# The first feed-forward block: down product in Strassen's scheme, and the modulation work spread over it

## What is computed

```python
def swiglu(h, w_gate, w_up, w_down):
    return (jax.nn.silu(h @ w_gate) * (h @ w_up)) @ w_down
...
    for l in range(DEPTH):
        shift1, scale1, gate1, shift2, scale2, gate2 = jnp.split(c_act @ ada_w[l] + ada_b[l], 6, axis=-1)
        if l == N_A_LAYERS:
            k_shift, k_scale = jnp.split(c_act @ kv_ada_w + kv_ada_b, 2, axis=-1)
...
        h = modulate(rms_norm(x, norm2_g[l]), shift2, scale2)
        x = x + gate2[:, None, :] * swiglu(h, ffn_w_gate[l], ffn_w_up[l], ffn_w_down[l])
```

## Time and profile before

| | us |
|---|---|
| median of 3 runs (1119.43 to 1123.12) | 1123.01 |
| the profiled execution | 1123.41 |
| its span | 1121.6 |
| PE busy in the span | 1059.0 (94%) |
| DVE busy in the span | 577.9 (52%) |
| first block on PE, from first gate product to last down product | 136.94 to 367.16 |
| second block on PE | 512.67 to 721.15 |

### The profile page before, as it was taken

The page is one execution under the profiler, slowest core; times in us unless marked ns, Lnnn a source line. Parts: engine busy times, 40 slices in busy tenths (PEclk is TensorE's granted clock), DMA queues, the critical chain, the costliest instruction groups (busy, mean ns, idle before and its releaser), DMA issues.

```text
span 1121.6 us, 21217 instructions
## 1 busy us (share of the span) xinstructions
PE 1059.0 (94%) x9229; PEld 910.9 (81%) x9229; DVE 577.9 (52%) x1112; ACT 295.6 (26%) x709; POOL 64.0 (6%) x84
## 2 busy tenths in 40 slices
PE   6878999999999999889999999999997899999997
PEld 4647888888888867678999999988886688887786
DVE  8986455344421727727766575335823551602632
ACT  6512410000000645623010000133322341202641
POOL 3010010110100100000000000000003000000000
PEclk9899999999999999999999999999998999999999
DMA  9995879999945334073544552443440003644220
GB/s 290 363 310 176 300 257 370 346 329 358 329 184 189 108 116 152 31 226 122 178 152 154 181 186 84 142 151 113 131 151 4 4 4 117 203 157 124 76 76 37
DMA packets 128742, 195.78 MB, mean 175 GB/s; under 512 B 4176, under 2 KB 114394, under 8 KB 122250
## 3 DMA queue, kind: packets, MB, share of 16 engines
q1 hardware_dynamic: 118218, 131.15, 36.7%
q0 software_dynamic: 10144, 62.92, 14.8%
q10 hardware_dynamic: 288, 0.36, 0.1%
HBM read 191.53 MB, written 1.05 MB: 172 GB/s over the span
## 4 chain that ended last, share of the span: by engine, by line
PE 82%; DVE 12%; ACT 3%; issue 2%; DMA 0%; SPq 0%; DVEq 0%; ACTq 0%
PE psum L743 48%; PE psum L1129 11%; PE psum L1215 7%; PE psum L1183 6%; DVE arena L1942 4%; PE psum L1018 2%; PE psum L1721 1%; ACT arena L2978 1%; DVE sq L1942 1%; DVE arena L1948 1%; DVE arena L2112 1%; PE psum L1696 1%; DVE arena L2206 1%; ACT sq L2978 1%; DVE arena L1945 1%
## 5 line engine op out<-in xcount | busy, mean ns | idle before, releaser
L2978 ACT ACTIVATE arena<-psum 128x512 f32<-128x512 f32 (+6 forms) x229 | 102.6, 475 | 574.6 <-PE psum L743 379.3
L743 PE MATMUL psum<-hT,ring 128*128 128x256 f32 x1072 | 239.4, 380 | 2.2 <-DVE hT L1948 1.3
L743 PEld LDWEIGHTS psum<-hT,ring 128*128 128x128 f32 x1072 | 201.3, 190 | 32.8 <-issue 6.5
L743 PE MATMUL psum<-arena 64*64 64x64 f32 (+6 forms) x2252 | 91.8, 252 | 16.4 <-issue 11.6
L1942 DVE TENSOR_TENSOR arena<-arena 128x512 f32<-128x512 f32 (+8 forms) x141 | 94.9, 696 | 11.3 <-PE psum L1183 8.6
L743 PE MATMUL psum<-hT,arena 128*128 128x256 f32 (+2 forms) x664 | 95.4, 323 | 4.9 <-DVE hT L1942 4.8
L743 PEld LDWEIGHTS psum<-hT,arena 128*128 128x128 f32 (+2 forms) x664 | 83.4, 180 | 16.5 <-issue 6.7
L743 PEld LDWEIGHTS psum<-arena 64*64 64x64 f32 (+3 forms) x2252 | 72.2, 150 | 30.3 <-issue 26.4
L743 PE MATMUL psum<-ring,arena 128*128 128x256 f32 (+2 forms) x288 | 73.3, 415 | 0.5 <-ACT arena L2978 0.5
L743 PEld LDWEIGHTS psum<-ring,arena 128*128 128x128 f32 x288 | 54.5, 190 | 18.1 <-issue 7.7
L1942 DVE TENSOR_TENSOR arena<-arena,psum 128x512 f32<-128x512 f32 (+2 forms) x56 | 30.7, 569 | 73.4 <-ACT arena L2978 41.1
(11 more groups left out here) (312 smaller groups left out, 1469.3 us busy)
## 6 DMA issues: line engine op xcount, KB each, us to landing
aring<-in_ada_w POOLq DMA_DIRECT2D x36, 1024.0 KB, 8.4
ring<-in_a_w_in SPq DMA_DIRECT2D x14, 1024.0 KB, 5.4
arena<-in_ffn_w_gate SPq DMA_DIRECT2D x12, 1024.0 KB, 5.4
arena<-in_ffn_w_up SPq DMA_DIRECT2D x12, 1024.0 KB, 8.3
ring<-in_ffn_w_down SPq DMA_DIRECT2D x11, 1024.0 KB, 6.8
ring<-in_ffn_w_gate SPq DMA_DIRECT2D x10, 1024.0 KB, 8.8
ring<-in_ffn_w_up SPq DMA_DIRECT2D x10, 1024.0 KB, 9.2
ring<-in_ada_w POOLq DMA_DIRECT2D x8, 1024.0 KB, 14.5
```

The lines of the kernel that those rows point to most:

```text
L743: return eng.matmul(dst, w, x, start=first, stop=last)
L2978: return eng.activation(dst, x, f, **k)
```

## The change

Layer 0 joins `HALVED`, with `FAST[0]` empty: its gate and up products stay whole (`whole_chunks`), and only its down product goes by Strassen's scheme, after all gates rather than between them. `swiglu` is gone from all engines. The calls of `ada_panel` are put at new places, 22 beside the gates and 14 beside the down product. Group 6 is summed in `acc` in place of `sq`. ACT copies the modulation columns out of PSUM (`take_columns`), and `ada_bias` adds the bias in SBUF. In both blocks the right-hand sums of the last three steps (8, 9, 10) are made by one `combine_hidden` behind the last step; before, the second block made those of steps 8 and 9 within step 10.

```diff
-        HALVED = (1,)
+        HALVED = (0, 1)
+        FAST = {0: (), 1: tuple(range(1, NDN))}
...
-                    n, nth, pool = unit_of(l, j), nth_of(l, j), "ab"[j % 2]
+                    n, nth, pool = unit_of(l, j), nth_of(l, j), "ab"[FAST[l].index(j) % 2]
...
+            ROWS_AT, COLUMNS_AT = {3: 3, 7: 4, 9: 5}, {4: 3, 8: 4, 10: 5}
...
+            def ada_beside_down(i, q):
+
+                if (i, q) == (2, 0):
+                    ada_rows(6)
+                if (i, q) == (2, 2):
+                    row_columns(6, row_late, "a")
+
+            swiglu_of_halves(0, 0, ada_beside, ada_beside_down)
...
                 for j in range(1, NDN):
+                    if j not in fast:
+                        for m in range(2):
+                            c = 2 * j + m
+                            combine_to(j + 1, m + 1)
+                            eng.wait_ge(*filled_at(("gu", l, c)))
+                            eng.wait_ge(done("silu_ready"), silus(l, c))
+                            tt(hid[:, c, :], hid[:, c, :], bank_of(("gu", l, c))[:, T:2 * T], ALU.mult)\
+                                .then_inc(*v.empties(("gu", l, c)))
+                            hid_done[0] = v.last
+                            beside(j, 1)
+                        combine_to(j + 1, 3)
+                        if j % 2 == 0 and j < NDN - 1:
+                            combine_hidden(l, [j - 2, j - 1])
+                        beside(j, 0)
+                        if j == NDN - 1:
+                            combine_down(l, 0)
+                            combine_down(l, 1)
+                        continue
...
-                combine_hidden(l, [NDN - 1])
+                combine_hidden(l, [8, 9, 10])
...
-                combine_down(l, 2)
-                combine_down(l, 3)
-                ahead = 4
+                ahead = 2
                 for i in range(KC // 2):
                     for d in range(ahead, min(3 * i + 6, DOWN_PANELS * KC // 2)):
                         combine_down(l, d)
+                        beside_down(i, d)
                     ahead = 3 * i + 6
+                    beside_down(i, None)
                     down_outputs(i)
...
-            def ada_beside(c):
-                for _ in range(2 if c < 14 else 1):
+            def ada_beside(j, n):
+                if n == 2 or j == 9:
+                    return
+                if n:
                     ada_panel()
-                if c in (7, 11, 15, 19):
-                    ada_bias({7: 3, 11: 4, 15: 5, 19: 6}[c])
-            swiglu(0, ada_beside)
+                elif j in (3, 6):
+                    ada_panel()
+                if n == 0 and j in (6, 10):
+                    ada_bias({6: 3, 10: 4}[j])
+
+            def ada_beside_down(i, d):
+                if d is not None:
+                    ada_panel()
+                else:
+                    for _ in range((0, 0, 1, 3)[i]):
+                        ada_panel()
+                    if i in (1, 3):
+                        ada_bias(5 if i == 1 else 6)
```

More of the change, by code:

```diff
@@ L2273, in combine_weights @@
                 g, u = slot(at), slot(at + 1)
-                s1, s2, s4 = [unit_sums(j)[:, x] for x in range(3)]
+                s1, s2, s4 = [unit_sums(l, j)[:, x] for x in range(3)]
                 if part == 1:
@@ L2340, in first_chunks, with swiglu_of_halves, combine_to @@
                 eng.wait_ge(*filled_at(("gu", l, 1)))
-                eng.wait_ge(done("silu_ready"), silu_base(l) + 2)
+                eng.wait_ge(done("silu_ready"), silus(l, 1))
                 tt(hid[:, 1, :], hid[:, 1, :], bank_of(("gu", l, 1))[:, T:2 * T], ALU.mult)\
                     .then_inc(*v.empties(("gu", l, 1)))
-            def swiglu_of_halves(l, h_base, behind):
+            def swiglu_of_halves(l, h_base, behind, beside=lambda j, n: None, beside_down=lambda i, d: None):
+                fast = FAST[l]
+                parts = [(j, part) for j in fast for part in range(1, 5)]
+                sent = [0]
+                def combine_to(j, part):
+                    while sent[0] < len(parts) and parts[sent[0]] <= (j, part):
+                        combine_weights(l, *parts[sent[0]])
+                        sent[0] += 1
@@ L2369, in swiglu_of_halves @@
+                    if ahead:
+                        combine_to(j + 1, 2)
                     eng.wait_ge(done("first_copied"), copy_of(l, j))
@@ L2390, in swiglu_of_halves @@
                     tt(hid[:, two, half_1], ps(p5), u2, ALU.add).then_inc(*v.empties(p5))
-                    if j < NDN - 2:
-                        combine_weights(l, j + 2, 1)
+                    if j + 2 in fast:
+                        if ahead:
+                            combine_to(j + 2, 1)
+                    beside(j, 1)
                     eng.wait_ge(*filled_at(p7))
@@ L3193, in swiglu_of_halves @@
                 for j in range(1, NDN):
+                    if j not in FAST[l]:
+                        for c in (2 * j, 2 * j + 1):
+                            eng.wait_ge(*filled_at(("gu", l, c)))
+                            act(hid[:, c, :], bank_of(("gu", l, c))[:, 0:T], ACT.Silu).then_inc(*s.signals("silu_ready"))
+                        beside(j)
+                        continue
                     nth, two = nth_of(l, j), slice(2 * j, 2 * j + 2)
```

214 lines of the change are left out of this document (98 added, 116 removed).

## The result

The changed kernel takes **1135.82 us** (median of 6 runs, 1134.93 to 1142.72) against 1123.46 before (6 runs, 1119.43 to 1124.66): 1.0122 times as long, 95% interval 1.0099 to 1.0144. Slower, as forecast, by 12.4 us where 9.3 were forecast. The profiled run took 1138.04, 2.2 above its median.

The account below looks back on a forecast made before the run. DVE was taken to bound the stretch behind the last gate chunk, delaying the `mem` load: 1123.4 + 6.9 (later projection) + 2.4 (clock) = 1132.7, less 0.4 for the median, 1132.3 us; range 1125 to 1141.

Parts of the forecast that it names:

- The walk of DVE: Row-by-row schedule of DVE against PE behind the last gate chunk: 75 us of DVE work against 68.8 + 1.9 on PE.
- S: Moment the first block's last gate chunk is full: 353.19 in the kernel before, forecast 289.1 after the change.
- The faster rival: Behind the last gate chunk DVE keeps up, PE never waits, all 7.2 us stay: 1115.8 us; chance 6%.
- The signs named: What the changed profile should show: PE's waits, the late `mem` load, projection near 380, DVE over 90% busy from 289 to 368.
- PE's first wait: After the first down product PE waits for DVE's sums of d = 0, from S + 1.3 to S + 6.0: 4.7 us.
- PE's second wait: Before the row of group 6 PE waits for panel 47, from S + 39.5 to S + 40.9: 1.4 us.
- The landings of panels 53 to 55: Transfers of the last modulation panels: 7 us each for 53 and 54, 5.8 for 55, used at S + 78.7.
- the quiet row: Profile row for a panel's landing on a quiet DMA: 5.8 us, at least 5.0.
- the crowded row: Profile row for a panel's landing in the crowded middle of the block: 8.2 us.
- The rival in which panels starve: Third rival: each landing behind S takes 8.2 us, `mem` lands at S + 95.9, 1143.4 us with the clock; chance 10%.
- The clock behind `mem`: After PE idles 8 us before the projection, half clock on 4.8 us of work: 2.4 us added, bounds zero and 4.
- The rest, priced at nothing: ACT's column copies, later hidden sums of steps 8 to 10 and first unit's banks in the second block: nothing, or 0.4 us.

Follow-up runs that it names:

- filler in the first wait: Changed kernel plus nine matmuls of 256 columns, result unused, on PE ahead of its wait for the sums of d = 0: 1133.41 us, ratio 1.0093.
- filler in front of `mem`: Changed kernel plus 20 matmuls of 256 columns, result unused, on PE between its last down product and its wait for `mem`: 1137.69 us, ratio 1.0136.
- the version with two places: Changed kernel with 28 modulation panels beside the gates, 8 behind the last, sums of d = 0 and 1 early, two panel buffers: 1116.11 us, ratio 0.9950.
- the one with three: Changed kernel with 28 panels beside the gates, early sums of d = 0 and 1, one weight buffer given as third panel buffer: 1115.67 us, ratio 0.9951.

## Why the prediction was right, and where its sizes were off

- **What bounds the block.** Right: DVE and the transfers, not PE. The walk of DVE held to about a microsecond up to panel 52 (forecast S + 62.5, used at S + 63.1). The faster rival, a DVE that keeps up, fell: from S on DVE or a landing is what is late, and PE waits twice.
- **The signs named.** The wait for `mem` was to be 6 to 10 us and was 10.29; POOL was to issue the load near 368 and did at 372.99; the projection was to start near 380 and did at 388.94; DVE was to be busy for over 90% of the stretch from 289 to 368 and was for 87% (69.0 of 79 us). The first three go the way that was forecast and beyond it; the fourth is missed, as DVE waited for landings.
- **S.** 289.1 forecast, 289.42 measured; PE's last down product ends 78.7 us behind it, where 76.7 was forecast, or 77.6 with the low clock. Gates, banks and places beside them were free, as priced.
- **PE's first wait.** 4.7 forecast, 4.55 measured. That it may bring the low clock was said, and it did, at 2.8 us. That nothing behind it moves was right for the load of `mem`, which was issued 81.2 us behind S with the clock kept up and 81.4 without.
- **PE's second wait, 1.4 us.** It did not come. The low clock had made PE late by more than that, so that panel 47 was ready. When the clock was kept up it came, at 2.27 us: the step was right for a PE at full clock, and the two terms, clock and second wait, were not independent.
- **The landings of panels 53 to 55: the term that was mis-sized.** "I take 5.8, and 7 for panels 53 and 54." They took 9.0, 8.5 and 7.3. The cause was named, the weight loads that d = 8 and d = 9 release, but its size was taken too near to the quiet row, though the crowded row gave 8.2. Panel 55, which had 5.8, also met such a load. `mem` was issued 83.6 us behind S and not 79.0: 4.5 us. Two other traces with the same order (filler in the first wait, filler in front of `mem`) have 81.2 and 81.4, with landings of 7.8, 7.1 and 6.2 us in one and 8.3, 6.1 and 5.2 in the other, where panel 52 took 6.4. So some 2.3 us of the miss are found in all three traces, and 2.2 in the profiled run of this kernel alone. The rival in which panels starve had 8.2 us for each landing: it came true for some of the last three, and not for the others.
- **The clock behind `mem`: also too small.** 2.4 was added, with 4 as the upper bound, after the one wait in the trace of before, where the clock rose 5 us behind the restart. Here it stayed at 0.50 until past 390, 12 us behind the restart, and the chain took 10.5 us in place of 6.3, with 0.7 more in the projection: 4.9 us, above the bound. What PE does there differs, too: ten matmuls of one column (20 records) with short groups on both sides, where the trace of before had 64 matmuls (128 records) in a row; whether that is the cause was not tried.
- **The load of `mem` itself.** 5.8 forecast, 5.4 measured.
- **The rest, priced at nothing.** Right: the shift is 16.3 us at 397.88 and 16.2 at 746.17, so ACT's copies and the second block's new order of the hidden sums cost nothing between them.
- **The sum.** From the profile: 0.3 (S) + 4.2 (`mem` in PE's hands at 378.42, 89.0 us behind S against 84.8) + 2.5 (clock) make 7.0 more than the 9.3 forecast, or 16.3 at 397.88; 1.7 come back behind 850, where the clock of the trace of before had fallen. Against the medians 12.4 - 9.3 = 3.1 us were missing. Landings of 2.3 and a clock of 2.5, less those 1.7, come to that, but this is an account and no measurement: the 1.7 is read from the two profiled executions alone, while the chain of 10.5 us stands also in the trace with filler in the first wait.
- **Two small slips in its sums.** 7.2 less 4.7 and 1.4 leaves 1.1 and not 1.4, and in the third rival S + 87 with 0.3 and 8.2 gives S + 95.5 and not 95.9. Nothing hangs on either.

## What to carry to other kernels

When an engine's work is moved behind a point at which its cover ends, add up that engine's work there and then follow the last transfer that hangs on it: here 14 panels behind S pushed a load that PE wants first out of PE's shadow, while the arithmetic saved was real and came out once six panels and 5 us of sums were moved to where DVE idles. A transfer that stands in a chain is priced by the row in which it shares the DMA, not by the quiet row. And a wait's price depends on who sets the end: in one order the same 4.5 us came out of a later wait of the same engine, and in another they cost 7.5 us, with the low clock behind them.

## What was not expected of the hardware

- The granted clock stayed at 0.50 for 12 us after PE had work again (378.4 to 390.3), while PE was shown busy, on groups of two to four matmuls of 128 columns, ten of one column and four of 512. Behind the first wait, on products of 128 columns one after another, it rose 6 us after the restart.
- The clock also fell without a wait of more than 0.83 us, in the same chain of one-column matmuls (0.66 from 360 to 365 in the version with two places; 1.00 in the one with three).
- With SP's weight loads held back, panels 53 to 55 (1 MB each) landed in 5.1 to 5.3 us. Beside those loads panels 53 and 54 took 9.0 and 8.5 us in one trace, 7.8 and 7.1 in the second and 8.3 and 6.1 in the third. The load of `mem`, also 1 MB, took 5.2 to 5.8 us in eleven of the thirteen traces and 6.7 and 7.4 in two, the 7.4 with no weight load beside it; why is open.
